# Gathering un-normed rows: the row scale moved into the selection, the shift added by a rank-one product

## The reference, cut to what matters

```python
mod = (silu(c) @ w_ada + b_ada)                       # sh1, sc1, gt1, sh2, sc2, gt2
x  = x + gt1 * (merged @ w_out)
h2 = rmsnorm(x, norm2_g) * (1.0 + sc2) + sh2
logits = h2 @ router_w + router_b                     # [256, 32]
top_v, top_e = top_k(logits, 4);  wts = softmax(top_v)
# per expert e, for the rows that chose it (padded blocks):
hgu = rows @ w_gate_up[e] + b_gate_up[e]              # 1024 -> 2048
act = (clip(up) + 1) * gate * sigmoid(1.702 * gate)
y   = act @ w_down[e] + b_down[e]                     # 1024 -> 1024
x = x + gt2 * sum(wts * y)
out = rmsnorm(x, final_g)
```

## Time and profile before

| what | us |
|---|---|
| median of 3 runs | 1346.19 |
| the profiled execution's own time | 1347.94 |
| its span in the profile | 1346.2 |
| TensorE, VectorE, ScalarE, GpSimd busy | 1320.4, 478.4, 300.9, 703.6 |
| read from memory | 482.40 MB |

### The profile page before, as it was taken

The page is one execution under the profiler, slowest core; times in us unless marked ns, Lnnn a source line. Parts: engine busy times, 40 slices in busy tenths (PEclk is TensorE's granted clock), DMA queues, the critical chain, the costliest instruction groups (busy, mean ns, idle before and its releaser), DMA issues.

```text
span 1346.2 us, 18076 instructions
## 1 busy us (share of the span) xinstructions
PE 1320.4 (98%) x6683; PEld 620.1 (46%) x6684; DVE 478.4 (36%) x862; ACT 300.9 (22%) x577; POOL 703.6 (52%) x430
## 2 busy tenths in 40 slices
PE   7999999999999999999999999999999999999996
PEld 3888545788844333333333333333333333333332
DVE  1160006355578324223233242333332333233332
ACT  2320004310023222222122122222222222222222
POOL 1000000010015777767777687777777777777771
PEclk9999999999999999999999999999999999999998
DMA  9735333499959999999999999999999999999995
GB/s 339 279 127 186 125 125 125 161 322 367 329 219 382 429 428 429 428 403 429 428 428 428 428 409 429 428 428 428 407 431 428 428 428 407 430 428 428 428 427 231
DMA packets 70818, 483.79 MB, mean 359 GB/s; under 512 B 7270, under 2 KB 7466, under 8 KB 44970
## 3 DMA queue, kind: packets, MB, share of 16 engines
q1 hardware_dynamic: 69250, 478.20, 86.8%
q0 software_dynamic: 1056, 3.93, 1.0%
q10 hardware_dynamic: 488, 1.33, 0.3%
HBM read 482.40 MB, written 1.05 MB: 359 GB/s over the span
## 4 chain that ended last, share of the span: by engine, by line
DMA 56%; PE 34%; POOL 4%; issue 3%; DVE 1%; SPq 1%; ACT 1%; POOLq 0%; DVEq 0%; ACTq 0%
DMA landing<-in_w_gate_up 41%; PE bank L1332 15%; DMA landing<-in_w_down 14%; PE bank L1341 6%; POOL gu_slot L566 3%; PE bank L1688 3%; PE bank L1738 3%; PE bank L1574 2%; DMA piece<-in_w_ada 2%; SPq L397 1%; PE bank L1660 1%; PE bank L1553 0%; PE bank L1478 0%; PE bank L1705 0%; SPq L391 0%
## 5 line engine op out<-in xcount | busy, mean ns | idle before, releaser
L566 POOL COPY gu_slot<-landing 128x2048 f32<-128x2048 f32 x246 | 458.8, 1895 | 145.0 <-issue 107.9
L1688 PE MATMUL bank<-gu_slot,xg 128*64 128x512 f32 x2304 | 509.4, 593 | 3.2 <-POOL gu_slot L566 2.8
L1688 PEld LDWEIGHTS bank<-gu_slot,xg 128*64 128x64 f32 x2304 | 164.3, 137 | 320.5 <-issue 298.4
L566 POOL COPY dn_slot<-landing 128x2048 f32<-128x2048 f32 x120 | 223.5, 1894 | 71.2 <-issue 53.6
L1738 PE MATMUL bank<-dn_slot,actT 128*64 128x512 f32 x1152 | 255.1, 595 | 0.0
L1332 PE MATMUL bank<-hT,piece 128*128 128x256 f32 x704 | 153.4, 379 | 0.0
L1738 PEld LDWEIGHTS bank<-dn_slot,actT 128*64 128x64 f32 x1152 | 79.5, 137 | 159.2 <-issue 158.7
L1332 PEld LDWEIGHTS bank<-hT,piece 128*128 128x128 f32 x704 | 133.4, 190 | 19.1 <-issue 1.1
L812 ACT ACTIVATE ypart<-bank 128x512 bf16<-128x512 f32 x105 | 62.7, 597 | 313.8 <-DVE bank L1241 260.2
L1230 DVE TENSOR_SCALAR bank<-bank 128x512 f32<-128x512 f32 x36 | 25.2, 700 | 283.6 <-PE bank L1688 283.6
L1241 DVE SCALAR_TENSOR_TENSOR bank<-bank,slot_w,gt2q 128x512 f32<-128x512 f32 x35 | 26.6, 759 | 238.8 <-PE bank L1738 238.8
(11 more groups left out here) (342 smaller groups left out, 986.8 us busy)
## 6 DMA issues: line engine op xcount, KB each, us to landing
landing<-in_w_gate_up SPq DMA_DIRECT2D x123, 2048.0 KB, 10.7
landing<-in_w_down SPq DMA_DIRECT2D x60, 2048.0 KB, 10.7
piece<-in_w_in SPq DMA_DIRECT2D x17, 2048.0 KB, 7.7
piece<-in_w_ada SPq DMA_DIRECT2D x12, 2048.0 KB, 13.2
gu_slot<-in_w_gate_up SPq DMA_DIRECT2D x10, 1024.0 KB, 7.1
dn_slot<-in_w_down SPq DMA_DIRECT2D x8, 1024.0 KB, 13.8
piece<-in_w_branch_a SPq DMA_DIRECT2D x2, 2048.0 KB, 9.3
piece<-in_w_branch_b SPq DMA_DIRECT2D x2, 2048.0 KB, 8.1
```

Source lines behind the costliest of these rows:

```text
L566: nc.gpsimd.tensor_copy(place, landing[j // 2 % 3][:, j % 2, :]).then_inc(there, 16)
L1688: ins = M(gu_bank[u][64 * q:64 * q + 64, :], xg[:, k % 4, 64 * (k // 4):64 * (k // 4) + 64], gu_slot[k][:, cols_], start=(k == 0), stop=(k ...
```

## The change

The scale by the inverse root is taken out of the rows that are gathered first, and the norm of tile 1 comes later.

- `take_wo` writes tile 0's raw rows to `u0` and tile 1's to `h2`; TensorE transposes these raw rows. The router's logits are `rs * (u @ router_w) + cb`, where `cb = sh2 @ router_w + router_b` is computed once (tiles `hc`). For this GpSimd stores `sh2` to memory and loads it back with one feature per partition (`shc`).
- `sel` holds `rs` instead of 1, so the gather scales the rows; `sh2` is added in the same sum by a product with a row of ones (`shift_rows`). The gather runs in two halves, each with a ranking product of its own (banks 4 and 3).
- `normed_rows(1)` comes after the selection. The counts, `br`, `te` and the transposes of `wts` stand behind pieces 0, 2 and 4 of the first `gate_up`; `router_weights` of both tiles stand behind `places_ready`.
- The sums for `gt2` come as one tile `ab7` in the layout of `gt2q`; `ab6` goes, and so do GpSimd's two copies.
- The second expert's unit 0 now lies over `yaT` and `ybT` and is issued after `wb3`; unit 1 waits on the rows and the gather; the first expert's last down piece (11) moves from beside `wb1` to behind `rp1`. There are fewer filler products (`keep_busy`).

```diff
-    + [("wb2", "V"), ("wb3", "V"), ("ab6", "V"), ("wo0", "V"), ("wo2", "V"), ("ab7", "V"), ("wo1", "V"), ("wo3", "V")]
+    + [("wb2", "V"), ("wb3", "V"), ("hc", "V"), ("wo0", "V"), ("wo2", "V"), ("ab7", "V"), ("wo1", "V"), ("wo3", "V")]
...
-                if kind in ("wa", "wb"):
+                if kind in ("wa", "wb") and (kind, i) != ("wb", 1):
                     wait_tile(sp, "o3")
                     load_expert_piece(0, 8 + 2 * (kind == "wb") + i)
...
                 load_expert_piece(0, 2 * q + 1)
+                if q == 3:
+                    wait_tile(sp, "wb3")
+                    land(E - 1, 0)
...
-            sp.wait_ge(h2_ready, 4)
-            sp.wait_ge(gate_ready, 3)
-            land(E - 1, 0)
-            wait_tile(sp, "rl1")
+            wait_tile(sp, "rp1")
+            load_expert_piece(0, 11)
+            sp.wait_ge(h2_ready, 2)
+            sp.wait_ge(added_ready, 2)
+            sp.wait_ge(gath_full, 1)
+            sp.wait_ge(gate_ready, 1)
             land(E - 1, 1)
...
+            wait_out(pool, "ab3")
+            pool.dma_start(shift_store[:], sh2[0:1, :]).then_inc(shift_out, 16)
+            pool.wait_ge(shift_out, 16)
+            pool.dma_start(shc[:], shift_store[0].rearrange("(k p) -> p k", p=P), allow_slow_non_contiguous=True).then_inc(shc_in, 16)
...
+            wait_tile(pool, "wo3")
+            for i in range(2):
+                step(nc.gpsimd.memset(ypart[i][:], 0.0), ypart_ready[i])
             pool.wait_ge(wts_ready, TT)
...
-                chain(V.tensor_copy(lg[:, t, 0:E], tile(f"rl{t}")[:, 0:E]), out_dve)
+                chain(V.scalar_tensor_tensor(lg[:, t, 0:E], tile(f"rl{t}")[:, 0:E], rs[:, t:t + 1], cb[:], ALU.mult, ALU.add), out_dve)
...
+                V.tensor_scalar(sel[:, t, :], slot_no[:], first_slot[:, t:t + 1], rs[:, t:t + 1], ALU.is_equal, ALU.mult).then_inc(
+                    sel_ready if t else sel0_ready, 1)
...
+            logits(0)
+            four_largest(0)
+            logits(1)
+            choose_slots(0, rank0_full, bank[4][:, 0:1])
+            four_largest(1)
+            choose_slots(1, rank1_full, bank[3][:, 0:1])
+            normed_rows(1, rows1, h2[:, 1, :], added_ready)
             wait_tile(dve, "rt")
...
+            def shift_rows(into):
+                for q in range(2):
+                    M(into[64 * q:64 * q + 64, :], ones[0:1, 0:SLOTS], sh2[0:1, 512 * q:512 * q + 512], start=False, stop=False)
...
+            wait_out(pe, "rl1")
+            pe.wait_ge(sel0_ready, 1)
+            gather(x_bank, 0)
             pe.wait_ge(chosen_ready, 2)
+            M(bank[3][:, 0:E], before[:], chosen[:, 1, 0, :], start=False, stop=True).then_inc(rank1_full, 1)
+            shift_rows(x_bank)
+            pe.wait_ge(sel_ready, 1)
+            gather(x_bank, 1).then_inc(gath_full, 1)
...
-            gate_up(16, 1, (block_tables, weight_transposes))
+            gate_up(16, 1, {0: rank_blocks, 2: block_tables, 4: weight_transposes})
```

More of the change, by code:

```diff
@@ L223, in hybrid_block @@
         over = sb("over", 188.25, [P, E, T // SLOTS])
-        rpart = sb("rpart", 152, [P, T])
+        rpart = sb("rpart", 98, [P, T])
+        u0 = sb("u0", 128, [P, D])
+        shc = small("shc", [P, KT])
+        rb2 = small("rb2", [1, E])
+        cb = small("cb", [P, E])
         first_used = small("first_used", [1, 1], I32)
@@ L1030, in take_sum, with take_gate @@
                     step(V.tensor_tensor(dst, tile(f"ab{r}")[:], dst, ALU.add), out_dve)
+            def take_gate():
+                wait_tile(dve, "ab7")
+                step(V.tensor_tensor(gt2q[:], tile("ab7")[:], gt2b[:], ALU.add), out_dve)
             def take_wa(i):
@@ L1060, in second_norm, with normed_rows @@
                 inverse_root(1, D, (x2ss_ready, 2 * t + 2), x2var_ready, x2root_ready, first=t)
+            def normed_rows(t, into, raw, signal):
                 for half in range(2):
                     cols_ = slice(512 * half, 512 * half + 512)
-                    step(V.scalar_tensor_tensor(h2[:, t, cols_], h2[:, t, cols_], rs[:, t:t + 1], sh2[:, cols_],
-                                                ALU.mult, ALU.add), h2_ready)
+                    step(V.scalar_tensor_tensor(into[:, cols_], raw[:, cols_], rs[:, t:t + 1], sh2[:, cols_], ALU.mult, ALU.add), signal)
             def weigh(r):
@@ L1171, in _ @@
             chain(V.tensor_reduce(blocks[:], over[:], AX.X, ALU.add))
+            step(V.tensor_scalar(first_used[:], blocks[0:1, 0:1], 1.0, None, ALU.add), first_count_ready)
+            step(V.tensor_copy(ranks[:].rearrange("p t e -> p (t e)"), tile("rt")[:, 0:TT * E]), out_dve)
             step(V.scalar_tensor_tensor(key_col[:], blocks_col[:], sorts_col[:], expert_no[:], ALU.mult, ALU.subtract))
@@ L1182, in _ @@
             step(V.tensor_scalar(by_place[:], iota[0:E, 0:E], place_col[0:E, :], None, ALU.is_equal))
-            step(V.tensor_scalar(first_used[:], blocks[0:1, 0:1], 1.0, None, ALU.add), first_count_ready)
             chain(V.tensor_scalar(place16[:], place_col[:], 16.0, 16.0, ALU.mult, ALU.add))
-            step(V.tensor_copy(ranks[:].rearrange("p t e -> p (t e)"), tile("rt")[:, 0:TT * E]), out_dve)
-            router_weights(1)
+            subtract_part(0, 1)
             wait_tile(dve, "br")
-            chain(V.scalar_tensor_tensor(dump[:], place_of[:], place_col[:], tile("br")[0:3 * E, 0:E], ALU.is_lt, ALU.mult,
+            chain(V.scalar_tensor_tensor(dump[:], place_of[:], place_col[:], tile("br")[0:3 * E, 4 * E:5 * E], ALU.is_lt, ALU.mult,
                                          accum_out=first_col[:]), out_dve)
-            subtract_part(0, 1)
             step(V.tensor_scalar(started[:], iota[0:3 * E, 0:MAXB + 1], first_col[:], None, ALU.is_ge))
@@ L1198, in _ @@
                  places_ready)
-            subtract_part(1, 1)
+            router_weights(0)
+            router_weights(1)
+            chosen_of_slots(first_slot[:, 0:1], first_slot[:, 1:2])
             def select(e):
@@ L1547, in _, with add_gate_parts @@
             attend(3)
+            def add_gate_parts():
+                ps = begin("ab7")
+                pe.wait_ge(modq_ready, 8)
+                for q in range(2):
+                    ins = M(ps[64 * q:64 * q + 64, :], ones[:, 0:64], modq[q][:], start=True, stop=True)
+                full(ins)
             def add_parts(r):
@@ L1565, in _ @@
                     by_feature(kind, cc, src)
-                    add_parts(r - 1)
+                    if r < 7:
+                        add_parts(r - 1)
                     r += 1
+            pe.wait_ge(late_in, 48)
+            pe.wait_ge(shc_in, 16)
+            ps = begin("hc")
+            for k in range(KT):
+                M(ps[0:1, 0:E], shc[:, k:k + 1], wr[:, k, :], start=(k == 0), stop=False)
+            full(M(ps[0:1, 0:E], ones[0:1, 0:1], rb[:], start=False, stop=True))
             pe.wait_ge(merged_ready, 4)
@@ L1576, in _ @@
                 if t == 0:
-                    add_parts(7)
+                    add_gate_parts()
+                    wait_out(pe, "hc")
+                    M(tile("hc")[:, 64:64 + E], ones[0:1, :], rb2[:], start=True, stop=True).then_inc(row_full, 1)
             pe.wait_ge(late_in, 48)
             pe.wait_ge(bias3_ready, 1)
-            for t in range(TT):
-                if t:
-                    keep_busy(tile("rp0"), 4)
-                for half in range(2):
-                    pe.wait_ge(h2_ready, 2 * t + half + 1)
-                    transposes(f"hh{2 * t + half}", h2, t, half)
+            pe.wait_ge(u_ready, 3)
+            transposes("hh2", h2, 1, 0)
+            pe.wait_ge(row_out, 1)
+            transposes("hh0", u0, None, 0)
+            transposes("hh1", u0, None, 1)
+            wait_out(pe, "wo2")
+            keep_busy(bank[7], 4)
+            pe.wait_ge(u_ready, 4)
+            transposes("hh3", h2, 1, 1)
+            for t in range(TT):
                 ps = begin(f"rp{t}")
-                keep_busy(ps, 3 if t else 7)
                 for r in range(2):
```

191 lines of the change are left out of this document (99 added, 92 removed), and 2 rows, old and new, of the table PLAN.

## The result

The changed kernel takes **1354.05 us** (median of 4 runs, 1352.34 to 1355.82) against 1346.16 us before (4 runs, 1345.65 to 1347.37): ratio 1.0055, 95% interval 1.0043 to 1.0066. It is slower, as forecast, but by 7.4 to 7.9 us and not by 3.4, and it lies outside the predicted range. The profiled execution took 1352.34 us, span 1350.6.

The account below looks back on a forecast made before the run. The start of the unbroken weight stream was taken as the bound: weights 4.9 us later, first copy 4.4, unit 3 landing 3.4 us late. Added to 1346.19, that gave 1349.6 us, range 1344.8 to 1352.4.

Parts of the forecast that it names:

- What bounds the kernel: The unbroken weight stream from 422 us on: its start waits for the weights, GpSimd's split and first copy, then unit 3.
- 1.7 us ahead: TensorE's lead over the transfers behind unit 3, from a first `gate_up` forecast 1.7 us earlier.
- The first `gate_up`: Its start after the router and gather: 413.7 us against 415.39 before, 1.7 us earlier, with 412.7 to 414.8 as ends.
- Piece 0 and the bias rows: Start of the first `gate_up`, now in front of `br`: 2.3 us, as before.
- From `br` to the weights: `br` 0.3 us, `first_col` to `of_block` 1.4, two `router_weights` 1.9; with the earlier steps, weights 4.9 us later.
- The split: GpSimd's split of `wts`, from the weights to the first copy: 3.3 us, with 2.7 and 3.8 as ends.
- One microsecond given back by the landing: Unit 3, issued 4.4 us late into an empty queue, lands in 7.78 us against 8.77, so 3.4 us late.
- the two halves: GpSimd's copies of the second expert's unit 0 and unit 3's issue: 3.95 us from the first copy, as before.
- The clock falls: Rival: fewer fillers before the first `gate_up` let TensorE's clock halve, some 3 us more before `br`: 1352.6 us; chance 7%.
- The shift row is late: Rival: store and load of `sh2` come after TensorE needs `shc`; 1356 us at 22 us each; chance 7%.
- The prefetch wins: Rival: first copy by about 416 us, the net 1 MB moved early gains 2.4 us: 1343.8 us; chance 12%.
- 1.7 + 1.1 us: TensorE's forecast lead plus its longest wait for copied weights: how much earlier a stream TensorE would allow.

Follow-up runs that it names:

- e2: The changed kernel with both `router_weights` moved in front of the wait for the counts: 1350.81 us, ratio 1.0031.
- e6: e5 with ScalarE's rounding of tile 1's rows behind `gx` and six fillers fewer: 1351.56 us, ratio 1.0026.
- e1: The changed kernel with eight filler products put back around the gather: 1352.74 us, ratio 1.0045.
- e3: The changed kernel with the edits of e1 and e2 together: 1346.95 us, ratio 1.0004.
- e5: e3 with VectorE's two `chosen_of_slots` of the first block moved in front of the wait for `br`: 1349.80 us, ratio 1.0024.
- e9: e5 with GpSimd's copies held until `places_ready` and `block_tables` behind piece 1 instead of piece 2: 1348.31 us, ratio 1.0011.
- e10: e9 with ScalarE's rounding behind `gx` and two fillers left: 1348.29 us, ratio 1.0010.
- e12: The kernel before without its eleven fillers between the second router product and the first `gate_up`: 1349.76 us, ratio 1.0019.
- e8: e6 with the second expert's unit 0 issued behind piece 11: 1349.19 us, ratio 1.0018.
- e11: e10 with the second expert's unit 0 issued behind piece 11: 1348.77 us, ratio 1.0015.
- e14: e10 with `subtract_part(1, 1)` before the wait for `te` and GpSimd reading its count before waiting for `places_ready`: 1347.59 us, ratio 1.0005.

## Why the prediction was wrong

*What bounds the kernel: right in the main, short in one thing.* The later weights held the split, the split the first copy, that the issue of unit 3, and the end followed nearly 1:1, as forecast (53.2, 56.9 and 60.7 us from w0, or 8.0, 7.9 and 7.7 late, and the end 7.3). That TensorE is close behind I had read as its lead ("1.7 us ahead"); in the changed kernel its first block was 1.7 us late instead, and it is the second bound. In e2 to e6 the end goes with TensorE's mark in the table, not with unit 3's.

*The first `gate_up`: 1.7 us earlier was forecast, 0.4 came* (w0 + 45.5 for 45.9). `gx` was out nearly as forecast (w0 + 42.6 for 42.4), and the two memsets did not hold VectorE (its three steps took 0.70 us each, for 0.69). From there the forecast had 1.8 us to the first `gate_up`; at 1.2 GHz the transposes took 1.13 and the zeroing products 1.88 us, 2.9 in all. That is 1.1 of the missing 1.3 us. The list itself was a little short as well: with the same order at full clock and the eight fillers (e1, e3, e5, e9) the first `gate_up` starts at w0 + 45.0, still 0.8 us behind the forecast, and how much of that is the fillers no run shows. e10 reaches w0 + 44.2, but with the rounding behind `gx`, which the forecast had in front.

*Piece 0 and the bias rows: 2.3 us was forecast, 3.95 came* (412.06 to 416.01). This is the step that failed. I knew the case as a rival, priced it at "some 3 us more, all of it before `br`", which is what came, and gave it 7%, because TensorE would be "still busy for about 6 of those 8 us". TensorE was in fact busy for 8.5 of the 9 us between 400 and 409 us, and the clock fell all the same. Even the rival's 1352.6 would have been 1.5 us short. The row that I needed was not in the trace of before: it shows a clock of 1.00 with fillers in the gaps, which says nothing of the clock without them. e12 shows it: without its fillers the kernel before loses 2.6 us as well.

*From `br` to the weights: right.* From `br`'s product at 416.01 to the second `wts_ready` at 419.77 it was 3.8 us, and 3.6 in the forecast (0.3, 1.4 and 1.9). With the two terms above that makes the weights 8.0 us late, not 4.9. *The split: right within 0.4* (3.73 us for 3.3, its upper end 3.8). The rule that the prediction named, from the Trainium skill, "SBUF — State Buffer", section "Who interferes with whom", holds for `wrest`: 1.31 us beside a subtraction of 1.23.

*One microsecond given back by the landing: wrong.* Unit 3 did land 1 us sooner after its issue, but that was no gain for the stream. Before, too, the queue had run low by then. Windows of one microsecond, before:

```profile
423.00:424.00 1.00, 1.00 (x6) 0.29 (x4) 1.00 (x1) 0.00 (x0) 1.00 (x1) 1.00 1.17 238
424.00:425.00 1.00, 1.00 (x8) 0.39 (x6) 1.00 (x2) 0.00 (x0) 1.00 (x2) 1.00 0.62 180
425.00:426.00 1.00, 1.00 (x8) 0.33 (x6) 1.00 (x1) 0.00 (x0) 1.00 (x1) 1.00 0.99 410
```

and after:

```profile
428.00:429.00 1.00, 1.00 (x8) 0.38 (x6) 1.00 (x1) 0.00 (x0) 1.00 (x1) 1.00 1.09 213
429.00:430.00 1.00, 1.00 (x8) 0.35 (x6) 0.24 (x2) 0.12 (x1) 1.00 (x2) 1.00 0.73 246
430.00:431.00 1.00, 1.00 (x12) 0.35 (x6) 1.00 (x2) 0.47 (x1) 1.00 (x2) 1.00 0.88 377
```

In the three microseconds that begin 0.6 to 0.7 us behind unit 3's issue 0.83 MB moved before and 0.84 after: the stream picks up alike in both, and so moves with that issue. The sum of the misses is 1.3 + 1.65 + 0.2 (from `br` to the weights) + 0.4 + 1.0, less 0.2 for the two halves, or 4.3 us; with the 3.4 forecast that is 7.7, unit 3's own shift, against 7.3 at the end of the profile.

*The rivals.* "The clock falls" happened. "The shift row is late" did not: the store landed in 5.7 us and the load of 1024 single elements in 4.0,

```profile
shc<-shift_store POOLq DMA_DIRECT2D x1, 4.0 KB, 4.0
```

far under the 12.1 of the earlier trace rows, and both were in some 25 us before TensorE read them, at 366.48. "The prefetch wins" named its own condition, weights some 7 us earlier or a first copy that does not wait for them. e2 to e6 met that condition, though only e6 had its first copy as early as the rival wanted (w0 + 46.1), and none of them won. Two things were missing in it: TensorE was not "1.7 + 1.1 us" ahead, and an early copy has a price, since it holds VectorE's steps, and through them TensorE. That price could be read in the trace of before, where the same steps fall under the first copies and TensorE happens not to wait for them:

```profile
420.74 1.73 DVE L1221 SCALAR_TENSOR_TENSOR slot_id<-slot_id,chosen 128x32 f32<-128x32 f32 x1
```

In the changed kernel, whose first copy starts behind them, such a step takes 0.19 us. Open stays what the prefetch is worth at an undisturbed clock, since the clock fell in e8 and e11.

## What to carry to other kernels

When a change takes fillers or idle-hiding work from TensorE, the trace of before can't show the clock without them: price the stretch that follows at 1.2 GHz as the main case, not as an accident (here it came in all three profiles without any of the eight fillers, and in e12). Where two bounds are nearly level, follow the later of the two marks (here the first block's end and the stream's restart), and compare both from a common event. And before an idle engine's large copy is moved earlier, list which short steps of the engine beside it will then fall under it.

## What the runs showed of the hardware

A GpSimd copy of 128x2048 floats, 1.9 us, holds some of VectorE's short steps until it ends, and lets others through. The list of e9, under six copies in a row:

```profile
422.21 0.18 DVE L1269 SCALAR_TENSOR_TENSOR slot_id<-bank,ranks 128x32 f32<-128x32 f32 x1
422.43 1.66 DVE L1271 SCALAR_TENSOR_TENSOR slot_id<-slot_id,chosen 128x32 f32<-128x32 f32 x1
...
425.96 1.79 DVE L1263 COPY wtcol<-wpart 128x6 bf16<-128x6 bf16 x1
```

The step with one of its inputs from PSUM takes 0.18 us, the one with two inputs from SBUF 1.66 (0.19 without a copy beside it), and a copy of six numbers per partition 1.79 (0.17 without). Among these short steps the size does not matter: each lasts until the copy beside it ends. The page cited above (the Trainium skill, "SBUF — State Buffer", "Who interferes with whom") says that whichever of the two issues first keeps the other out for its whole instruction, and lists two SBUF inputs among the cases; the rows of `slot_id` agree, and e14's first copy shows the other direction. I had used the rule for GpSimd alone.

The same list of TensorE instructions ran its first piece at 2.4 GHz in e6 and at 1.2 GHz in e8 (1.94 and 3.68 us), after a stretch from 406 us on without visible gaps in either; e10 and e11 are a second such pair (1.94 and 3.47). Without the fillers the clock of this stretch is not settled by TensorE's own list. In both pairs only the issue of unit 0 differs, and each kernel has one profile, so whether that or chance decides is open.
